# Keys and values of the memory for the last layer: projected in the first mixer instead of the latent-attention stage

## The chip, the cores and the metric

The kernel runs on one core of a Trainium2 chip. The metric is the device time of one execution in microseconds (us), from the median of several runs; less is better. The core has TensorE (PE, matrix products), VectorE (DVE), ScalarE (ACT), GpSimd (POOL) and SyncE (SP, which here only issues DMAs). They run in parallel, each through its own instructions in order, and wait for each other on semaphores.

## The reference

The reference is four transformer layers on a 256 x 1024 activation in float32. The two of the first block: an even mixer (attention with dilated branches and eight heads of 64, beside a state-space scan with a GLU), an odd mixer (gated linear recurrence), a SwiGLU behind each. The two of the second block: latent attention and grouped-query attention, each with a memory attention beside it, a SwiGLU behind each. What the change moves is the memory part of the last layer (i = 1):

```python
mem_n = _rmsnorm(mem, mem_norm)
kv = (mem_n @ w_kv).reshape(B, M, 2, MEM_HEADS, MEM_HEAD_DIM)
k = _rmsnorm(kv[:, :, 0], k_norm)
v = kv[:, :, 1]
```

`mem` (256 x 1024) and `w_kv` (1024 x 1024) are inputs: neither depends on any layer, so k and v can be computed at any time before the last attention.

## The kernel before

Every product is made in three matmuls (`mm3`, L404 to L406): weights and activations are split into a high part and a remainder (`WH` and `WL`; `HTh` and `HTl`, `YAh` and `YAl`, `CTh` and `CTl`), and high x high, high x low and low x high are added in PSUM. All weights stand in one array of chunks of 128 x 2048, in the order of `plan()`. SyncE loads them into three buffers `RAW`; ACT copies a chunk into `WH` (L1015), VectorE subtracts for `WL` (L1588), and there are three buffers of each. On ACT and VectorE `feed(c)` splits the chunks up to c + 3; the split of chunk n waits on ACT until TensorE has used chunk n - 3, and on VectorE until ACT has done its part. `rows_mm` on TensorE goes over the chunks of a matrix (24 matmuls of 512 columns in a full one) and calls a `hook` behind each; `rows_mm` on ACT and VectorE calls `feed`, then the hook.

There is no scheduler: the order on each engine is the order of the code. In the first mixer the chunks are ev_u, ev_q, ev_k, ev_v, and the state scan goes in four groups q = 0 to 3 through the hooks. On VectorE `seg_a(q)` rotates (L1866 to L1874) and then calls `skip(q - 1)` (L1853), and `seg_b(q)` makes the next group's angle table (L1836, L1840), eight scans (L1888, L1889) and four products W (L1893 to L1896). On TensorE `seg_a(q)` is `c_h(q - 1)` (L569 to L574; it waits for the W of that group) and `seg_b(q)` is `b_u(q + 1)` (L557; it waits until VectorE has read the last group's PSUM). On ACT `seg_a` and `seg_b` make angles and sines. Groups 2 and 3 lie within `attention0`: a loop of ten steps in which TensorE makes scores of head h (L621), turns P of head h - 1 and multiplies head h - 2 (L646), with `glu` at step 6; ACT has exp (L1295), gelu at step 4 and the GLU's tanh at step 7. Behind it comes ev_out.

The latent-attention stage runs `mla_a`, `mla_b`, `mla_c`, then `mem10` and `mem11` (keys and values of the memory for the last layer) between the products of the latent projections qb2, qb0 and kvb0; `mem_rows(1)` turns the 256 x 1024 memory on TensorE first, `mem_hi(1)` and `mem_lo(1)` split it into HTh and HTl, `gain_turn` turns the normed keys into `KM`. `qb2` waits for `CTl`, which `c_lo` on VectorE makes behind the feed of mla_c. `power` on GpSimd (L2248) makes each inverse root, in the fixed order of `NAMED_RSTD`.

## Time and profile before

| | us |
|---|---|
| median of 3 runs | 1373.48 (1372.35 to 1377.26) |
| the profiled execution | 1378.56 |
| its span, first to last instruction | 1376.8 |
| TensorE busy in it | 1285.7 |
| VectorE busy | 819.8 |
| ScalarE busy | 680.4 |
| GpSimd busy | 52.0 |
| mean granted clock of TensorE, as a share of 2.4 GHz | 0.971 |

The profile is one execution, and its rows carry the times below. In a timeline a row is a run of like instructions on one engine: start, length, engine, line, operation, output and input, count, and in brackets the idle time before it with who ended it. L12 is line 12 of the kernel. The ends of matmuls are modelled, so the distance of starts is the better measure of their pace. The granted clock is 1.00 at 2.4 GHz and 0.50 at 1.2 GHz.

### The profile page before, as it was taken

What the parts mean: (1) busy time and instruction counts of PE and PEld (TensorE: products, weight loads), DVE (VectorE), ACT (ScalarE), POOL (GpSimd) and SP (SyncE); (2) the same over time, 40 slices, a digit from 0 to 9 for tenths busy, and PEclk for the clock granted to TensorE, in tenths of its full rate; (3) what the DMA queues carried; (4) which work ended last, traced back from release to release, by engine and by line L of the source; (5) the groups of instructions that cost most, each with busy time, mean ns of one, the idle gap of its engine ahead of it and who ended that gap; (6) DMA issues with size and microseconds to landing.
All of it is one profiled execution on the core that took longest, in us unless ns stands there. A gap on an engine that the chain in (4) does not pass through costs nothing.

```text
span 1376.8 us, 15928 instructions
## 1 busy us (share of the span) xinstructions
PE 1285.7 (93%) x6374; PEld 1053.0 (76%) x6374; DVE 819.8 (60%) x1132; ACT 680.4 (49%) x1087; POOL 52.0 (4%) x67
## 2 busy tenths in 40 slices
PE   6888899999998989999999889999999969999998
PEld 5666688888786778888787668788887857788887
DVE  7793565563686675664567543766545664666643
ACT  6444354443568664443488733544435553544431
POOL 0110000000000010000012100000000100000000
PEclk9887999999999999999999899999999989999999
DMA  8330255555543446555455203555554511465551
GB/s 309 120 108 1 95 199 184 185 178 198 188 180 99 177 157 214 189 188 183 155 203 198 88 7 123 184 183 183 184 184 164 183 62 61 153 213 184 184 183 62
DMA packets 31962, 216.62 MB, mean 157 GB/s; under 512 B 3840, under 2 KB 4224, under 8 KB 6672
## 3 DMA queue, kind: packets, MB, share of 16 engines
q1 hardware_dynamic: 30240, 210.29, 43.7%
q0 software_dynamic: 1360, 4.78, 1.1%
q8 instruction: 50, 0.82, 0.2%
q10 hardware_dynamic: 288, 0.52, 0.1%
q14 instruction: 24, 0.20, 0.0%
HBM read 214.54 MB, written 1.05 MB: 157 GB/s over the span
## 4 chain that ended last, share of the span: by engine, by line
PE 76%; DVE 12%; ACT 8%; issue 3%; DMA 1%; POOL 1%; SPq 0%; DVEq 0%; ACTq 0%
PE PS L404 22%; PE PS L406 22%; PE PS L405 22%; PE PS L410 4%; DVE WL L1588 3%; ACT WH L1015 3%; PE PS L676 2%; PE PS L699 2%; ACT JK L1127 1%; ACT HTh L1028 1%; DVE HTl L1602 1%; DMA RAW<-in_w 1%; POOL st L2248 1%; PE PS L557 0%; DVE YG L1633 0%
## 5 line engine op out<-in xcount | busy, mean ns | idle before, releaser
L1588 DVE TENSOR_TENSOR WL<-RAW,WH 128x2048 fp32r<-128x2048 f32 (+1 forms) x200 | 451.1, 2260 | 397.9 <-ACT WH L1015 397.8
L1015 ACT ACTIVATE WH<-RAW 128x2048 fp32r<-128x2048 f32 (+1 forms) x200 | 377.3, 1891 | 443.9 <-PE PS L406 442.2
L404 PE MATMUL PS<-WH,HTh 128*128 128x512 f32 (+2 forms) x1008 | 399.7, 397 | 24.1 <-DVE WL L1588 13.4
L406 PE MATMUL PS<-WH,HTl 128*128 128x512 f32 (+2 forms) x1008 | 393.0, 390 | 0.0
L405 PE MATMUL PS<-WL,HTh 128*128 128x512 f32 (+2 forms) x1008 | 392.4, 389 | 0.0
L404 PEld LDWEIGHTS PS<-WH,HTh 128*128 128x128 f32 x1008 | 191.0, 190 | 64.7 <-DVE WL L1588 25.0
L406 PEld LDWEIGHTS PS<-WH,HTl 128*128 128x128 f32 x1008 | 190.6, 189 | 39.8
L405 PEld LDWEIGHTS PS<-WL,HTh 128*128 128x128 f32 x1008 | 191.2, 190 | 36.7
L404 PE MATMUL PS<-WH,YAh 128*128 128x512 f32 x386 | 153.2, 397 | 1.0 <-DVE WL L1588 0.6
L405 PE MATMUL PS<-WL,YAh 128*128 128x512 f32 x386 | 151.1, 391 | 0.0
L406 PE MATMUL PS<-WH,YAl 128*128 128x512 f32 x386 | 150.9, 391 | 0.0
L404 PEld LDWEIGHTS PS<-WH,YAh 128*128 128x128 f32 x386 | 73.1, 189 | 16.3 <-DVE WL L1588 1.1
L406 PEld LDWEIGHTS PS<-WH,YAl 128*128 128x128 f32 x386 | 73.0, 189 | 15.6
L405 PEld LDWEIGHTS PS<-WL,YAh 128*128 128x128 f32 x386 | 73.1, 189 | 14.7
L2248 POOL TENSOR_TENSOR st<-st,mh 128x2 f32<-128x2 f32 (+4 forms) x33 | 36.2, 1099 | 913.0 <-DVE st L1618 913.0
L1028 ACT ACTIVATE HTh<-PS,cst 128x128 fp32r<-128x128 f32 (+1 forms) x144 | 40.8, 396 | 37.5 <-PE PS L410 37.5
L1602 DVE SCALAR_TENSOR_TENSOR HTl<-PS,cst,HTh 128x128 fp32r<-128x128 f32 (+1 forms) x144 | 41.0, 359 | 14.4 <-ACT HTh L1028 13.9
L1028 ACT ACTIVATE YAh<-PS 128x512 fp32r<-128x512 f32 x38 | 21.6, 584 | 21.5 <-PE PS L410 21.5
L410 PE MATMUL PS<-ident,X 128*128 128x128 f32 x128 | 18.7, 286 | 10.1 <-DMA X<-in_x 5.5
L410 PEld LDWEIGHTS PS<-ident,X 128*128 128x128 f32 x128 | 15.1, 146 | 14.4 <-issue 9.6
L410 PE MATMUL PS<-ident,Z 128*128 128x128 f32 (+1 forms) x124 | 19.3, 291 | 6.3 <-DVE Z L1723 3.6
L410 PEld LDWEIGHTS PS<-ident,Z 128*128 128x128 f32 (+1 forms) x124 | 14.5, 142 | 11.9 <-issue 4.6
(349 smaller groups left out, 1358.2 us busy)
## 6 DMA issues: line engine op xcount, KB each, us to landing
RAW<-in_w SPq DMA_DIRECT2D x197, 1024.0 KB, 4.9
BC<-in_rows POOLq DMA_DIRECT2D x4, 512.0 KB, 3.9
YG<-in_mem POOLq DMA_DIRECT2D x4, 512.0 KB, 5.0
X<-in_x SPq DMA_DIRECT2D x2, 512.0 KB, 6.0
BC<-in_s SPq DMA_DIRECT2D x1, 512.0 KB, 12.7
BB<-in_s SPq DMA_DIRECT2D x1, 512.0 KB, 12.4
YG<-in_s SPq DMA_DIRECT2D x1, 512.0 KB, 13.1
out_x<-X SPq DMA_DIRECT2D x2, 256.0 KB, 2.1
```

The costliest lines, as they stand in the source:

```text
L404: e.matmul(out, ah, bh, start=start, stop=False)
L405: e.matmul(out, ah, bl, start=False, stop=False)
L406: return e.matmul(out, al, bh, start=False, stop=stop)
L410: return e.transpose(out, src, ident[0:p, 0:p])
L676: tk = e.matmul(PS[:, h % 2, 256 * t:256 * t + 256], q[:, 128 * t:128 * t + 128], k[:, 0:256], start=i == 0, stop=i == len(parts) - 1)
L699: tk = e.matmul(PS[:, b, o:o + 128], PT[:, h % 2, kt, 128 * t:128 * t + 128], heads[h]["v"][kt], start=kt == 0, stop=kt == 1)
L1015: e.activation(WH[:, c % NW, w], RAW[:, c % NR, w], ACT.Copy).then_inc(S.hi, 1)
L1028: return e.activation(out, src, ACT.Copy, scale=scale)
L1127: e.activation(JK[:, d * i:d * i + d], z[:, d * i:d * i + d], ACT.Square, accum_out=st[:, SO[name] + nh * n + i:SO[name] + nh * n + i + 1] ...
L1588: e.tensor_tensor(WL[:, c % NW, w], RAW[:, c % NR, w], WH[:, c % NW, w].bitcast(f32), SUB).then_inc(S.lo, 1)
L1602: return e.scalar_tensor_tensor(out, src, gain, hi.bitcast(f32), MUL, SUB)
L2248: e.tensor_tensor(st[:, at:at + n], st[:, at:at + n], mh[:, 0:n], ALU.pow).then_inc(S.rs, 1)
```

## The change

The two projections of the last layer's memory leave the latent-attention stage. In the first mixer `mem` is loaded into the buffer of x (`MX` is X, which has been turned by then and is loaded again later), turned in four rounds of four transposes through one PSUM bank (`mem_round`) behind ev_k, ev_v's first chunk and ev_v, and split into YAh and YAl; `mem10` and `mem11` follow ev_v. The scan's groups 2 and 3 move from the first steps of `attention0` into the hooks of these two, and `attention0` begins when they are through, with gelu ahead of its first exp and glu at step 3 instead of 6. In the latent-attention stage what used `mem10` and `mem11` goes, qb0 comes directly behind qb2, and some banks and buffers change. Buffers W, cosT and PT0 of the scan now lie over KM, VM and BB, which saves the room that KM and VM take up earlier.

The diff, cut to its core. The plan, buffers, and TensorE's part:

```diff
+    for i in range(2):
+        add(f"mem1{i}", nat("w_mem_kv_2", 1, [(512 * i, 512)]))
...
     add("mla_c", nat("mla_w_in_2", 0, [(704, 512)]))
-    add("mem10", nat("w_mem_kv_2", 1, [(0, 512)]))
...
-    add("mem11", nat("w_mem_kv_2", 1, [(512, 512)]))
...
+            MX, KZ1 = X, BC[:, :].rearrange("p (t n) -> p t n", t=2)
...
-            PT0 = sb("A0PT", [128, 2, 2, 256])
+            PT0 = BB[:, :, :, :].rearrange("p r (b q) s -> p r b (q s)", b=2)
...
-        KM, VM = sb("KM", [128, 2, 4, 256]), sb("VM", [128, 2, 2, 512])
...
             def glu():
...
+                e.wait_ge(S.gout, GT["memk1"] + 2)
...
             def attention0():
                 def step(h):
-                    if h == 0:
-                        seg_b(2)
-                    elif h == 1:
-                        seg_a(3)
+                    if h == 1:
+                        gain_turn(KZ1, "memk1", (4, 5), lambda jp: e.wait_ge(S.bread, 4) if jp == 0 else None)
...
-                        c_h(3)
-                    elif h == 6:
...
-                    if h == 0:
-                        e.wait_ge(S.pairs, 6)
-                    if h > 1:
+                    if h < 2:
+                        e.wait_ge(S.kz, h + 1)
+                    else:
...
                 def turn_p(h):
...
-                        e.wait_ge(S.ev, 8)
+                        e.wait_ge(S.vm, h + 1)
...
+            def mem_round(j):
+                if j == 0:
+                    e.wait_ge(S.c_mem, 32)
+                    e.wait_ge(S.k0, 1)
+                else:
+                    e.wait_ge(S.mlo, 2 * j)
+                four(6, MX, j).then_inc(S.mt, 1)
...
+                    mem_round(0)
...
             def behind_v(ci):
...
                     pairs(Qn, (0, 1), q_ready)
+                    mem_round(1)
...
                     pairs(Kn, (0, 1), k_ready)
+                    mem_round(2)
...
             rows_mm(PLAN["ev_v"], 4, 8, 512, HT, (2, 3), v_free, behind_v)
+            mem_round(3)
+            def mem10_ready(k, t):
+                if k == 0:
+                    e.wait_ge(S.pairs, 5 + t)
+                if t == 0:
+                    e.wait_ge(S.mlo, k + 1)
+            def mem11_free(k, t):
+                if k == 0:
+                    e.wait_ge(S.ev, 7 + t)
+            MT = (YAh, YAl)
+            rows_mm(PLAN["mem10"], 4, 8, 512, MT, (0, 1), mem10_ready, lambda ci: seg_a(3) if ci else seg_b(2))
+            rows_mm(PLAN["mem11"], 4, 8, 512, MT, (2, 3), mem11_free, lambda ci: c_h(3) if ci else None)
...
-            mem_rows(1)
             rows_mm(PLAN["mla_c"], 4, 8, 512, HT, (0, 1), evacuated("za"))
...
-            rows_mm(PLAN["mem10"], 4, 8, 512, HT, (0, 1), mem10_ready)
...
             rows_mm(PLAN["qb2"], 3, 3, 512, CQ, (2, 3), qb2_ready)
+            rows_mm(PLAN["qb0"], 3, 3, 512, CQ, (0, 1), evacuated("zc"))
             gain_turn(ZC, "zm", (5, 6))
-            rows_mm(PLAN["mem11"], 4, 8, 512, HT, (0, 1), mem11_free)
...
-            gain_turn(ZD, "memk1", (4, 5), lambda jp: e.wait_ge(S.gout, GT["qmt"] + 1) if jp else e.wait_ge(S.ctl, 5))
-            rows_mm(PLAN["qb0"], 3, 3, 512, CQ, (2, 3), evacuated("z2"))
-            rows_mm(PLAN["kvb0"], 2, 2, 512, CK, (0, 1), kvb0_free, keep=S.kv)
+            e.wait_ge(S.ctl, 5)
+            rows_mm(PLAN["kvb0"], 2, 2, 512, CK, (2, 3), evacuated("z2"), keep=S.kv)
...
             def ready2(h):
-                if h == 4:
+                if h < 2:
+                    e.wait_ge(S.z, ZEV["vt0"] + h + 1)
+                elif h == 4:
```

ACT's part:

```diff
+            def mem_round(j):
+                e.wait_ge(S.mt, j + 1)
+                for k in (2 * j, 2 * j + 1):
+                    tk = copy(YAh[:, k, :], PS[:, 6, 256 * (k % 2):256 * (k % 2) + 256], col("mem_norm_2", k))
+                tk.then_inc(S.mhi, 1)
...
+                    mem_round(0)
+                    mem_squares(0, MX, yq[:, :, :].rearrange("p a b -> p (a b)"))
...
             def behind_v(ci):
...
                     pairs(1, QT, (0, 1), 0.125)
+                    mem_round(1)
...
                     pairs(2, KT, (0, 1))
+                    mem_round(2)
...
+            mem_round(3)
+            rows_mm(PLAN["mem10"], lambda ci: seg_a(3) if ci else seg_b(2))
+            e.wait_ge(S.used, PLAN["mem10"][1] + 1)
+            e.wait_ge(S.rs, RSTD["mem1"])
+            mem_k((0, 1), KZ1)
+            e.wait_ge(S.kz, 2)
+            head_squares("memk1", [KZ1[:, t, :] for t in range(2)], 4, 128, X[:, 0, :])
+            rows_mm(PLAN["mem11"])
+            e.wait_ge(S.used, PLAN["mem11"][1] + 1)
+            mem_v(1, (2, 3))
...
             def attention0():
                 def step(h):
...
-                        seg_b(2)
+                        gelu()
...
-                        seg_a(3)
+                        gain_turn("memk1", lambda j: KM[:, 1, j:j + 2, :], col("memk_norm_2", 1), (4, 5))
...
-                        gelu()
-                    elif h == 7:
...
-                    elif h == 8:
+                    elif h == 6:
...
-            e.wait_ge(S.hsq, HSQ["zk"] + 2)
-            e.wait_ge(S.c_mem, 64)
-            mem_squares(1)
             feed(PLAN["mla_c"][0])
             z_evac("zc", PLAN["mla_c"][1], (0, 1), ZC, 512, True)
-            mem_hi(1)
             feed(PLAN["mla_c"][1])
...
             c_turn(2, (2, 3), 3)
-            e.wait_ge(S.msq, 4)
+            c_turn(3, (4,), 4)
+            e.wait_ge(S.hsq, HSQ["zk"] + 2)
             head_norm("zm", two(ZC), 4, 128, "zc")
...
-            feed(PLAN["mem10"][0])
-            c_turn(3, (4,), 4)
-            e.wait_ge(S.used, PLAN["mem10"][1] + 1)
-            e.wait_ge(S.rs, RSTD["mem1"])
-            mem_k(1, (0, 1), ZD)
-            feed(PLAN["mem10"][1])
-            e.wait_ge(S.kz, 4)
-            e.wait_ge(S.hsq, HSQ["pe"] + 2)
-            head_squares("memk1", two(ZD), 4, 128)
             z_evac("z2", PLAN["qb2"][0], (2, 3), ZB)
             feed(PLAN["qb2"][0])
-            e.wait_ge(S.hsq, HSQ["memk1"] + 8)
+            e.wait_ge(S.hsq, HSQ["pe"] + 2)
             head_norm("qp", two(ZB), 8, 64, "z2")
+            z_evac("z0", PLAN["qb0"][0], (0, 1), ZD)
+            feed(PLAN["qb0"][0])
...
             gain_turn("qmt", lambda j: QMT[:, j:j + 2, :], gq[:, 1:2], (5, 6))
-            feed(PLAN["mem11"][0])
-            e.wait_ge(S.used, PLAN["mem11"][1] + 1)
-            mem_v(1, (0, 1))
-            feed(PLAN["mem11"][1])
...
-            gain_turn("memk1", lambda j: KM[:, 1, j:j + 2, :], col("memk_norm_2", 1), (4, 5))
-            z_evac("z0", PLAN["qb0"][0], (2, 3), ZA)
-            feed(PLAN["qb0"][0])
-            z_evac("zk0", None, (0, 1), ZC, kv=1)
+            z_evac("zk0", None, (2, 3), ZC, kv=1)
```

VectorE's part (`seg_a` has a new argument `between`, called ahead of `skip`):

```diff
+                if ed == 1 and t == 0:
+                    e.wait_ge(S.c_xr, 32)
...
+            def mem_round(j):
+                e.wait_ge(S.mhi, j + 1)
+                for k in (2 * j, 2 * j + 1):
+                    rest(YAl[:, k, :], PS[:, 6, 256 * (k % 2):256 * (k % 2) + 256], YAh[:, k, :], col("mem_norm_2", k)).then_inc(S.mlo, 1)
...
+                if between:
+                    between()
...
-                    seg_a(1)
+                    seg_a(1, mem_first)
+            def mem_first():
+                mem_round(0)
+                mem_var(0, "mem1")
             def behind_v(ci):
...
+                    mem_round(1)
...
-                    seg_a(2)
+                    seg_a(2, lambda: mem_round(2))
+            def behind_mem11(ci):
+                if ci == 0:
+                    seg_b(3)
+                    head_var("memk1", 4, 128)
+                else:
+                    skip(3)
+                    scaled("memk1", [KZ1[:, t, :] for t in range(2)], 4, 128)
...
             rows_mm(PLAN["ev_v"], behind_v)
+            mem_round(3)
+            rows_mm(PLAN["mem10"], lambda ci: seg_a(3) if ci else seg_b(2))
+            rows_mm(PLAN["mem11"], behind_mem11)
...
             def attention0():
                 def step(h):
-                    if h == 0:
-                        seg_b(2)
-                    elif h == 1:
-                        seg_a(3)
-                    elif h == 2:
-                        seg_b(3)
-                    elif h == 3:
-                        skip(3)
+                    if h == 2:
+                        gelu_lo()
...
-                        gelu_lo()
-                    elif h == 8:
...
-                    elif h == 9:
+                    elif h == 7:
...
             feed(PLAN["mla_c"][0])
-            mem_lo(1)
             feed(PLAN["mla_c"][1])
...
             c_lo(2, (2, 3), 3)
+            c_lo(3, (4,), 4)
             head_var("zm", 4, 128)
...
-            feed(PLAN["mem10"][0])
-            c_lo(3, (4,), 4)
-            feed(PLAN["mem10"][1])
-            head_var("memk1", 4, 128)
             feed(PLAN["qb2"][0])
...
-            scaled("memk1", two(ZD), 4, 128)
...
                 rope("qp", ZB[:, t, :], 8, 64, t, tg[:, 0, :, :, :], RP, RQ)
-            feed(PLAN["mem11"][0])
-            feed(PLAN["mem11"][1])
             feed(PLAN["qb0"][0])
...
-            scaled("n0", two(ZA), 4, 128)
+            scaled("n0", two(ZD), 4, 128)
```

GpSimd's part:

```diff
+            e.wait_ge(S.turn, turn_n(0, 1, 1))
+            e.wait_ge(S.rowsq, 2)
+            for t in range(2):
+                e.dma_start(MX[:, t, :], A["mem"][128 * t:128 * t + 128, :]).then_inc(S.c_mem, 16)
...
-            e.wait_ge(S.k0p, 1)
+            power("mem1", 16, 2)
+            power("memk1", SO["memk1"], 8)
+            e.wait_ge(S.mt, 4)
+            e.wait_ge(S.msq, 2)
+            e.wait_ge(S.hsq, HSQ["memk1"] + 8)
+            for t in range(2):
+                e.dma_start(X[:, t, :], A["x"][128 * t:128 * t + 128, :]).then_inc(S.c_xr, 16)
+            e.wait_ge(S.gturn, GT["memk1"] + 2)
...
-            mem_rows()
...
-            power("mem1", 16, 2)
...
-            power("memk1", SO["memk1"], 8)
```

## Rows read from the trace of the kernel before

**Rows 1.** The page's parts 1 and 4: TensorE, and the chain that ended last.
```profile
PE 1285.7 (93%) x6374; PEld 1053.0 (76%) x6374; DVE 819.8 (60%) x1132; ACT 680.4 (49%) x1087; POOL 52.0 (4%) x67
PE 76%; DVE 12%; ACT 8%; issue 3%; DMA 1%; POOL 1%; SPq 0%; DVEq 0%; ACTq 0%
```
**Rows 2.** Windows: length, busy time of each engine, granted clock, DMA share.
```profile
53.90:62.60 8.70, 8.63 (x104) 7.29 (x105) 8.56 (x16) 1.92 (x4) 0.80 (x1) 0.50 0.42 148
83.40:146.10 62.70, 46.27 (x416) 37.02 (x415) 37.80 (x89) 28.57 (x69) 0.00 (x0) 0.72 0.10 35
698.95:700.62 1.67, 1.67 (x19) 1.67 (x17) 0.97 (x2) 1.47 (x3) 0.62 (x1) 1.00 0.99 422
699.00:762.10 63.10, 56.99 (x282) 46.90 (x281) 44.74 (x90) 51.46 (x128) 13.23 (x9) 0.98 0.50 181
714.46:725.44 10.98, 10.98 (x49) 9.04 (x49) 8.57 (x21) 9.72 (x31) 2.30 (x2) 1.00 0.31 108
```
**Rows 3.** Timeline of TensorE in the state scan: start, length, operation, idle before.
```profile
53.85 1.22 PE L557 MATMUL PS<-uT,BBe 32*128 32x128 f32 x8 [5.31 <-DVE JK L1872]
58.01 1.08 PE L543 MATMUL PS<-CFo,BC 128*32 128x32 f32 x64
60.47 0.63 PE L404 MATMUL PS<-WH,HTh 128*128 128x512 f32 x1
60.89 0.63 PE L405 MATMUL PS<-WL,HTh 128*128 128x512 f32 x1
91.02 1.22 PE L557 MATMUL PS<-uT,BBe 32*128 32x128 f32 x8 [2.63 <-DVE JK L1872]
109.14 0.65 PE L569 MATMUL PS<-uT,K 32*32 32x128 f32 x8 [2.40 <-DVE W L1896]
146.11 0.78 PE L404 MATMUL PS<-WH,YAh 128*128 128x512 f32 x1
```
**Rows 4.** Timeline of ACT and VectorE, one round of the scan from 83.48 on.
```profile
83.48 1.91 ACT L1015 ACTIVATE WH<-RAW 128x2048 fp32r<-128x2048 f32 x1 [1.74 <-PE PS L406]
85.43 2.29 DVE L1588 TENSOR_TENSOR WL<-RAW,WH 128x2048 fp32r<-128x2048 f32 x1 [0.34 <-ACT WH L1015]
87.64 0.68 DVE L1866 TENSOR_TENSOR YG<-PS,cosT 128x512 f32<-128x512 f32 x1
91.00 0.69 DVE L1874 TENSOR_TENSOR YG<-YG,JK 128x512 f32<-128x512 f32 x1
92.00 0.42 DVE L1836 TENSOR_SCALAR sinT<-cosT 128x512 f32<-128x512 f32 x1
97.68 0.69 DVE L1896 TENSOR_TENSOR W<-YG,cosT 128x512 f32<-128x512 f32 x1
```
**Rows 5.** Timeline of ACT at gelu, within the first attention.
```profile
116.92 1.06 ACT L1215 ACTIVATE yq<-yq 128x1024 f32<-128x1024 f32 x1
119.08 1.28 ACT L1295 ACT_TABLE_LOAD   x1
```
**Rows 6.** Timeline of the latent-attention stage around mem10, and at qb1.
```profile
711.80 1.26 ACT L1028 ACTIVATE Z<-PS,st 128x512 f32<-128x512 f32 x2 [3.47 <-PE PS L406]
714.46 0.47 PE L404 MATMUL PS<-WH,HTh 128*128 128x512 f32 x1 [1.82 <-DVE HTl L1602]
720.03 1.65 DVE L1602 SCALAR_TENSOR_TENSOR YAl<-PS,cst,YAh 128x256 fp32r<-128x256 f32 x4
763.44 0.99 PE L404 MATMUL PS<-WH,YAh 128*128 128x512 f32 x1
```
**Rows 7.** Timeline of the same stage: norm and rotation of the q parts.
```profile
734.42 1.14 ACT L1121 ACTIVATE JK<-Z 128x512 f32<-128x512 f32 x2
736.77 1.27 DVE L2158 TENSOR_REDUCE st<-JK 128x8 f32<-128x512 f32 x2
738.33 3.27 POOL L2248 TENSOR_TENSOR st<-st,mh 128x16 f32<-128x16 f32 x1 [4.64 <-DVE st L1618]
744.64 0.69 DVE L2121 TENSOR_TENSOR Z<-Z,st 128x512 f32<-128x512 f32 x1
```

More of the change, by code:

```diff
@@ L725, in gain_turn, with mem_rows @@
                     four(bks[jp], src, jp, lambda j, t: e.wait_ge(S.nz, NZ[name] + t + 1) if j == 0 and jp == 0 else None).then_inc(S.gturn, 1)
-            def mem_rows(i, free=None):
-                e.wait_ge(S.c_mem, 32 * (i + 1))
+            def mem_rows(free):
+                e.wait_ge(S.c_mem, 64)
                 for t in range(2):
                     for k in range(8):
-                        if t == 0 and k % 2 == 0 and free:
+                        if t == 0 and k % 2 == 0:
                             free(k // 2)
@@ L951, in tfree2 @@
             def tfree2(h):
-                if h == 0:
-                    e.wait_ge(S.z, ZEV["vt0"] + 2)
-                elif h == 3:
+                if h == 3:
                     e.wait_ge(S.gout, GT["qt1"] + 2)
@@ L1856, in dve, with seg_a @@
             rotated = {}
-            def seg_a(q):
+            def seg_a(q, between=None):
                 C, Sn, A0, A1 = slots(q)
@@ L2076, in mem_norm @@
                 scaled("memk0", [KZ[:, t, :] for t in range(2)], 4, 128)
[L2078 removed]
+            wide_mm(PLAN["od_out"], 3, after=(lambda: mem_var(1, "mem0"), mem_norm))
             ffn(1, 3)
```

91 lines of the change are left out of this document (39 added, 52 removed).

## Prediction

> **What bounds the kernel now.** I read the page first: TensorE is busy for 93% of the span and carries 76% of the chain that ended last [rows 1]. A step that only moves TensorE's work can pay only where TensorE stands still, or runs at the lower of its two clocks. So I cut the span into stages. From 83.4 to 146.1 (the rest of the state scan, and the first attention laid over it) TensorE is busy 46.3 us of 62.7 at a granted clock of 0.72; from 699.0 to 762.1 (the latent-attention stage up to its first products) it is busy 57.0 of 63.1 at 0.98 [rows 2]. In the first there are 16 us of idle to fill, in the second hardly any. Then the timelines, for who is late. In the scan TensorE waits for VectorE: 5.31 us ahead of 53.85, 2.63 ahead of 91.02, 2.40 ahead of 109.14 [rows 3]. VectorE's own order there is a weight remainder (WL), six rotation steps, the table, the scans, four products W, all in one line with no gap [rows 4]. VectorE is the pacer of this stage, and that decides what moved matmuls find there.
>
> **What moves.** Two projections of 48 matmuls each, 11.0 us apiece [rows 2], 16 transposes of `mem` (1.7 us, the same group) and 8 for memk1 (0.9 at the same rate): 24.5 us of TensorE time at full clock. Nothing is saved in total, apart from waits and clock. Both ends must be walked through.
>
> **The scan stage, step by step.** Rates: a 512-column matmul is 0.23 us at 2.4 GHz (10.98 / 48) and 0.43 at 1.2 GHz (60.47 to 60.89) [rows 2, 3]; a chunk is 24 of them, 5.5 or 10.3 us. b_u took 4.2 at the low clock (53.85 to 58.01 [rows 3]), c_h about as much, so 2.1 to 2.3 at the high one. WH takes 1.9, WL 2.2 [rows 4].
> - Two memory rounds of 4 transposes stand ahead of the end of ev_v, 0.5 each: everything from 83.4 on is 1.0 later. ACT gets 4.0 more ahead of Kn's evacuation (squares and two copies); the rope of K on GpSimd then ends near 78.4 against a first use at 84.3, so that is hidden. It would cost at once if Kn came 6 us late.
> - `mem_round(3)` on TensorE waits for the remainders of round 2, and VectorE has these behind WL (86.4) and the rotation (87.64 to 91.69 before [rows 4], so 88.6 to 92.6): they end at 93.5. TensorE has run out at 88.5. This is a new wait of 5.0 us. An idle of 5.31 before left the granted clock at 0.50 for the next 8.7 us [rows 2, 3]. So mem10's first chunk starts at 94.0 and pays 20 matmuls at 0.43 and 4 at 0.23: it ends at 103.5, where 99.5 would be undisturbed.
> - Now the order on VectorE bites. `rows_mm` calls `feed` ahead of the hook, and feed of that chunk splits the chunk three places on, which needs the buffer that this chunk frees. So seg_b(2), which started at 92.0 before, queues behind WH and WL: 103.5 + 4.2 = 107.7, and with its 6.4 us (92.00 to 98.37 [rows 4]) it ends at 114.1. TensorE does b_u(3) and the next chunk meanwhile (2.3 + 5.5, to 111.3) and waits 2.8 for W.
> - c_h(2) 2.3, mem11's first chunk 5.5: 121.9. Again WH and WL (126.1), then seg_b(3), which has no table (1.1 of the 6.4), 5.3: 131.4. TensorE's last chunk ended at 127.4, so it waits 4.0. c_h(3) starts at 131.4; before, it started at 109.14 [rows 3]: 22.3 later.
> - From c_h(3) to the first ev_out matmul are 37.0 us now (109.14 to 146.11 [rows 3]). After the change heads 0 to 3 no longer lie ahead of it (about 4 us more), and gelu, its copy and a table load (116.92 to 120.36, 3.4 us [rows 5]) stand ahead of the first exp; against that no scan step and no gelu interrupt the heads. I take 38, between 33 and 42.
> Scan stage: 22.3 + 1 = **23.3 later**. That is almost all that was moved in: the idle is not filled, it is pushed back.
>
> **The latent-attention stage.** `mem_rows` is gone, so mla_c ends at 709.9 in place of 711.6. What mem10 and mem11 covered is now bare.
> - qb2 needs CTl. ACT evacuates zc (1.2 [rows 6]), splits a chunk (1.9), copies; VectorE has WL in front of c_lo (2.2 and 0.8, half of the four in 1.65 [rows 6]): 709.9 + 1.2 + 1.9 + 2.2 + 0.8 = 716.1, with TensorE out of work at 711.2. A new wait of 4.9, and the clock at 0.50 again: 18 matmuls at 0.43 end qb2 at 723.9.
> - The rotated q parts: evacuation 1.1, WH 1.9, WL 2.2 (the squares, 1.1, run beside it), reductions 1.3, and then the 7.1 from POOL's start to the last product (738.2 to 745.3, of which POOL has 3.3 [rows 7]): 737.5. TensorE has qb0 (4.7, its first matmuls slow), 10 transposes and 12 matmuls (4.0) until 732.6: a second wait of 4.9, of which the trace before shows nothing, because mem11 lay over it.
> - 16 transposes and 12 matmuls follow at the low clock to 746.2. Then ACT: evacuation 1.1, WH 1.9, QTn 1.2, half of KTn 0.6: qb1 starts at 751.0. Before it started at 763.44 [rows 6]: 12.4 gained, and 1.5 more, since qb1 ran its first matmuls at the low clock before (0.99 for the first, against 0.47 for the one at 714.46 [rows 6]).
> This stage: **13.9 earlier**, not 26.
>
> **Sum.** 23.3 - 13.9 = 9.4. The profiled execution took 1378.56 us (span 1376.8), so 1388.0 in its own terms; the median before is 1373.48, 5.1 below that execution, and I put the difference on it: **1383**.
>
> Edits with no price: the DMA of `mem` goes from GpSimd at about 25 us, when 16 transposes of X are done, into X; needed at 67. X is read again and BC's gain row comes only after KZ1 is turned, near 141; first use is in the add behind ev_out, beyond 185. Each of these 1 MB loads costs nothing unless its issue slips by 40 us: GpSimd waits inside power("memk1") until 132, and only these two DMAs are queued behind it. The DMA engines are at 0.10 in the stage [rows 2]. SyncE's queue sees the same chunks in another order. The added waits (kz, vm, gout of memk1, vt0) fall on steps that come later anyway in this schedule.
>
> **The rivals.**
> B, the clock costs nothing. My sum has four stretches at the low clock. Without them mem10's chunk ends 4.0 earlier and c_h(3) takes 2.0 less (stage +17.3), and in the latent stage 3.6 on qb2 and 4.0 behind the second wait go (21.5 earlier): 4.2 net gain, 1369. For it: the wait of 1.82 ahead of 714.46 left the clock at 1.00 [rows 2, 6]. Against it: 5.31 and 2.63 did not, the stage as a whole is at 0.72 [rows 2, 3]. The Trainium skill (TensorE: Matmul & The Clock Gate, What's actually happening) counts the ramp as under 1% of a typical span and advises not to fit to a number of slow matmuls. By that rule rival B's time would hold; the trace shows 8.7 us at 0.50 after one such wait, which speaks against it here.
> C, faster: the heads, no longer cut up by scan steps, run at TensorE's pace. The place is c_h(3) to ev_out. Before, this stage had 16.4 us of idle [rows 2]; if all of it takes in moved work, the stage grows by 24.5 - 16.4 = 8.1 and the sum is 8.1 - 13.9 = -5.8, 1368, and with B's clock in part 1363. It decides once the 38 us shrink below 22. Against it: gelu, glu, tanh and ten head steps still hang on ACT, and the scans still hang on WL. The Trainium skill (Perfetto Trace Analysis, Optimization Strategy) says that interleaving regimes with different contended engines may improve performance. By that rule C would be the outcome; the trace has VectorE without a gap in just this stretch, so I hold it unlikely.
> D, more waits tip the clock. The 2.8 us ahead of c_h(2) is as long as the 2.63 that did it before: c_h(2) 2.1 and mem11's chunk 2.2 more. In the heads VectorE has WL and two steps of glu in front of head 5's mask, about 2.5 of idle and a slow tail, 4 more: 1391.
>
> **How the numbers follow.** Forecast 0.50 (own range 1377 to 1389), B 0.20, C 0.12, D 0.18. Range 1367 to 1394: it takes in B, D, most of C and both ends of the 38. About 0.5% (6.9 us) is what can be told from no change: 1366.6 to 1380.3. Slower: 0.40 of the forecast and all of D, 0.58. Same: 0.10 of the forecast, B, 0.30. Faster: 0.12.
>
> **What would show it.** On TensorE a wait near 5 us ahead of the transposes of round 3, and waits of some 3 and 4 ahead of c_h(2) and c_h(3), all released by VectorE; seg_b(2)'s scans directly behind a WL; c_h(3) near 131. The first ev_out matmul near 169 to 170. In the later stage two waits near 5 us, ahead of qb2 and of the transposes of the q parts, each followed by a clock of 0.50; the stage shorter by 14 at its end. I am wrong if seg_b(2) starts before mem10's first chunk ends, if ev_out starts before 160, or if either of the two later waits is missing.

## Result and profile after

| | before | after |
|---|---|---|
| median, same chip (4 runs each) | 1375.14 us | 1390.35 us (1388.71 to 1390.78) |
| ratio | 1 | 1.011, 95% interval 1.0086 to 1.0133 |
| profiled execution, its span | 1378.56, 1376.8 | 1390.78, 1389.0 |
| TensorE busy, mean granted clock | 1285.7, 0.971 | 1291.2, 0.965 |

The change costs 15.2 us by the medians and 12.2 between the spans of the two profiled executions. First TensorE's timeline of the kernel after (start, length, operation, idle before and who ended it), as rows 3 and 6 show it of before:

```profile
92.06 1.11 PE L412 MATMUL PS<-ident,X 128*128 128x128 f32 x4 [4.63 <-DVE YAl L1613]
92.82 0.77 PE L406 MATMUL PS<-WH,YAh 128*128 128x512 f32 x1
100.96 0.73 PE L559 MATMUL PS<-uT,BBe 32*128 32x128 f32 x8
111.79 0.65 PE L571 MATMUL PS<-uT,K 32*32 32x128 f32 x8 [2.73 <-DVE VM L1916]
131.32 0.65 PE L571 MATMUL PS<-uT,K 32*32 32x128 f32 x8 [4.54 <-DVE VM L1916]
140.21 0.84 PE L412 MATMUL PS<-ident,Kn 128*128 128x128 f32 x3 [1.89 <-ACT Kn L1323]
162.50 1.11 PE L412 MATMUL PS<-ident,YG 128*128 128x128 f32 x4 [3.08 <-ACT BB L1038]
175.34 0.78 PE L406 MATMUL PS<-WH,YAh 128*128 128x512 f32 x1
...
745.64 0.77 PE L406 MATMUL PS<-WH,YAh 128*128 128x512 f32 x1 [5.27 <-DVE YAl L1613]
762.84 0.30 PE L412 MATMUL PS<-ident,Z 128*64 128x128 f32 x1 [2.83 <-DVE Z L2149]
765.77 3.41 PE L412 MATMUL PS<-ident,Z 128*64 128x128 f32 x15 [2.63 <-DVE Z L2149]
777.45 0.77 PE L406 MATMUL PS<-WH,YAh 128*128 128x512 f32 x1 [2.19 <-ACT KTn L1038]
```

Every wait of the scan ends on a VectorE operation. Read from the top: round 3's transposes wait for the remainders of round 2; the moved chunk starts; c_h(2) and c_h(3) (the operations that begin with `uT,K`) wait for W, which now lies in VM's memory. c_h(3) starts at 131.32 (109.14 before [rows 3]), ev_out at 175.34 (146.11 before [rows 3]). So the first ev_out matmul is 29.2 later. VectorE's timeline says why:

```profile
84.95 2.29 DVE L1599 TENSOR_TENSOR WL<-RAW,WH 128x2048 fp32r<-128x2048 f32 x1
91.14 0.87 DVE L1613 SCALAR_TENSOR_TENSOR YAl<-PS,cst,YAh 128x256 fp32r<-128x256 f32 x2
103.07 2.29 DVE L1599 TENSOR_TENSOR WL<-RAW,WH 128x2048 fp32r<-128x2048 f32 x1 [8.11 <-ACT WH L1025]
105.28 0.42 DVE L1854 TENSOR_SCALAR sinT<-KM 128x512 f32<-128x512 f32 x1
106.42 0.42 DVE L1908 TENSOR_TENSOR_SCAN YG<-s,YG 128x128 f32<-128x128 f32 x1
...
123.39 2.29 DVE L1599 TENSOR_TENSOR WL<-RAW,WH 128x2048 fp32r<-128x2048 f32 x1 [5.17 <-ACT WH L1025]
125.59 0.42 DVE L1908 TENSOR_TENSOR_SCAN YG<-s,YG 128x128 f32<-128x128 f32 x1
```

The engine that paces the scan stands still for 8.11 and 5.17 us. What it waits for is a half of a weight chunk that may be split only when the moved chunk has freed its buffer, and the table and the scans of group 2 (105.28, 106.42) and group 3 (125.59) are queued behind that. Before, the table of group 2 ran at 92.00 [rows 4].

Windows of the kernel after (length; busy time of PE, PEld, DVE, ACT, POOL; granted clock; DMA share and GB/s): the scan up to c_h(3), from there to ev_out, the stretch behind the wait of 3.08, and the one behind the wait of 5.27.

```profile
83.40:131.32 47.92, 35.05 (x284) 27.83 (x283) 32.07 (x53) 21.99 (x41) 0.00 (x0) 0.87 0.26 89
131.32:175.34 44.02, 36.78 (x241) 29.80 (x241) 17.61 (x48) 20.05 (x57) 5.25 (x4) 0.69 0.24 84
162.50:180.10 17.60, 16.93 (x60) 13.96 (x61) 4.76 (x14) 5.53 (x17) 0.00 (x0) 0.50 0.01 5
745.60:750.20 4.60, 4.55 (x11) 3.62 (x12) 2.98 (x11) 1.78 (x12) 2.29 (x2) 0.51 0.65 228
```

The heads run at 0.69, and from 162.5 to 180.1 TensorE is busy 16.9 of 17.6 us at the low clock. The latent-attention stage, from its first matmul to out0's first, went from 146.15 (681.39 to 827.54) to 129.95 (710.65 to 840.60): 16.2 shorter. 29.2 - 16.2 = 13.0, against 12.2 between the spans.

### The profile page after: what moved, and what is told of

It is laid out like the page before. It is cut to its first block, busy times and chain, and to the rows that moved or that the text cites. A ratio compares the mean times of both kernels' runs of the same rounds, so it can differ in the third digit from the quotient of the medians.

```text
span 1389.0 us, 15929 instructions
## 1 busy us (share of the span) xinstructions
PE 1291.2 (93%) x6374; PEld 1057.3 (76%) x6374; DVE 819.5 (59%) x1132; ACT 680.7 (49%) x1086; POOL 55.4 (4%) x69
## 4 chain that ended last, share of the span: by engine, by line
PE 77%; DVE 11%; ACT 7%; issue 2%; POOL 1%; DMA 0%; SPq 0%; DVEq 0%; ACTq 0%
PE PS L406 23%; PE PS L408 23%; PE PS L407 23%; PE PS L412 4%; DVE WL L1599 3%; ACT WH L1025 3%; PE PS L675 2%; PE PS L698 1%; ACT HTh L1038 1%; ACT JK L1137 1%; POOL st L2268 1%; DVE HTl L1613 1%; DMA RAW<-in_w 0%; PE PS L645 0%; DVE YG L1644 0%
## 5 line engine op out<-in xcount | busy, mean ns | idle before, releaser
L406 PE MATMUL PS<-WH,HTh 128*128 128x512 f32 (+2 forms) x976 | 387.2, 397 | 20.2 <-DVE WL L1599 12.6
L408 PE MATMUL PS<-WH,HTl 128*128 128x512 f32 (+2 forms) x976 | 380.7, 390 | 0.0
L407 PE MATMUL PS<-WL,HTh 128*128 128x512 f32 (+2 forms) x976 | 380.4, 390 | 0.0
L406 PEld LDWEIGHTS PS<-WH,HTh 128*128 128x128 f32 x976 | 185.0, 190 | 59.4 <-DVE WL L1599 23.3
L406 PE MATMUL PS<-WH,YAh 128*128 128x512 f32 x418 | 168.9, 404 | 7.8 <-DVE YAl L1613 5.3
L407 PE MATMUL PS<-WL,YAh 128*128 128x512 f32 x418 | 166.1, 397 | 0.0
L408 PE MATMUL PS<-WH,YAl 128*128 128x512 f32 x418 | 165.9, 397 | 0.0
L406 PEld LDWEIGHTS PS<-WH,YAh 128*128 128x128 f32 x418 | 81.0, 194 | 25.3 <-DVE WL L1599 5.5
L408 PEld LDWEIGHTS PS<-WH,YAl 128*128 128x128 f32 x418 | 80.6, 193 | 17.5
L407 PEld LDWEIGHTS PS<-WL,YAh 128*128 128x128 f32 x418 | 81.0, 194 | 16.5
L412 PE MATMUL PS<-ident,X 128*128 128x128 f32 x144 | 21.8, 291 | 12.8 <-DMA X<-in_x 5.1
L412 PEld LDWEIGHTS PS<-ident,X 128*128 128x128 f32 x144 | 17.4, 148 | 17.6 <-issue 7.6
L412 PE MATMUL PS<-ident,Z 128*128 128x128 f32 (+1 forms) x116 | 18.3, 298 | 8.3 <-DVE Z L2149 5.5
```

Source lines behind the costliest of these rows:

```text
L406: e.matmul(out, ah, bh, start=start, stop=False)
L407: e.matmul(out, ah, bl, start=False, stop=False)
L408: return e.matmul(out, al, bh, start=False, stop=stop)
L412: return e.transpose(out, src, ident[0:p, 0:p])
```

## Experiments

All marks below are starts on TensorE in the profiled execution. Four orders that could be to blame were changed one by one (e1 to e4), then the clock and the heads were tested. All edits are against the changed kernel, but for e12's, which is against the kernel before. `finish`, named below, is the step behind four heads in which TensorE turns their result; the first stands within head 5.

| kernel | median us | c_h(2) | c_h(3) | ev_out | c_h(3) to ev_out |
|---|---|---|---|---|---|
| before | 1375.14 | 98.51 | 109.14 | 146.11 | 37.0 |
| after | 1390.35 | 111.79 | 131.32 | 175.34 | 44.0 |
| e1 scan ahead of the split | 1382.01 | 108.39 | 121.73 | 166.22 | 44.5 |
| e2 glu behind mask 5 | 1388.38 | 111.38 | 130.84 | 174.25 | 43.4 |
| e3 remainders ahead | 1382.92 | 104.87 | 124.25 | 167.84 | 43.6 |
| e4 latent copies ahead | 1386.09 | 111.10 | 130.65 | 174.62 | 44.0 |
| e5 all four | 1373.60 | 102.65 | 115.99 | 159.89 | 43.9 |
| e6 matmuls in the scan's waits | 1384.54 | 109.10 | 127.10 | 169.18 | 42.1 |
| e7 glu late | 1392.07 | 110.83 | 128.81 | 175.51 | 46.7 |
| e8 matmuls at finish | 1384.88 | 110.53 | 128.56 | 169.37 | 40.8 |
| e9 heads ahead | 1384.57 | 112.16 | 131.74 | 168.91 | 37.2 |
| e10 what paid, together | 1363.50 | 102.36 | 116.79 | 149.71 | 32.9 |
| e11 and the latent waits | 1358.40 | 102.32 | 116.75 | 148.15 | 31.4 |
| e12 before, matmuls in waits | 1369.08 | 97.52 | 109.85 | 140.35 | 30.5 |

**e1: the order on VectorE.**

```diff
-            rows_mm(PLAN["mem10"], lambda ci: seg_a(3) if ci else seg_b(2))
-            rows_mm(PLAN["mem11"], behind_mem11)
+            seg_b(2)
+            feed(PLAN["mem10"][0])
+            seg_a(3)
+            feed(PLAN["mem10"][1])
+            behind_mem11(0)
+            feed(PLAN["mem11"][0])
+            feed(PLAN["mem11"][1])
+            behind_mem11(1)
```

> The changed kernel with one thing reordered: on VectorE and ScalarE the scan steps of groups 2 and 3 are issued ahead of the weight split that the moved chunk triggers, not behind it. TensorE's instructions are untouched. Theory (the split is in front of the scan in VectorE's order, and it waits for the moved chunk): seg_b(2) runs at about 95 to 101, c_h(2) loses its wait of 2.7, and c_h(3) starts when TensorE has done the last moved chunk, near 122.5 and with no wait, where it was 131.3; the first ev_out matmul comes near 166.5 (was 175.3), and the time is about 1381.5 against the changed kernel's 1390.4. Rival (the moved work itself, 24.5 us of matmuls, is what fills the stage): c_h(3) stays within 2 us of 131 and the time within 2 of 1390. Rival (the heads behind it are the bound): c_h(3) moves, but ev_out by less than 3.

Measured: 1382.01 (ratio to before 1.0045, 1.0029 to 1.0061). TensorE's and VectorE's timelines of e1:

```profile
108.39 0.43 PE L571 MATMUL PS<-uT,K 32*32 32x128 f32 x8
121.73 0.43 PE L571 MATMUL PS<-uT,K 32*32 32x128 f32 x8
...
96.67 0.42 DVE L1911 TENSOR_TENSOR_SCAN YG<-s,YG 128x128 f32<-128x128 f32 x1
102.47 2.29 DVE L1602 TENSOR_TENSOR WL<-RAW,WH 128x2048 fp32r<-128x2048 f32 x1 [0.56 <-ACT WH L1025]
```

Both waits are gone, no bracket stands at either c_h, the wait of VectorE for WH is 0.56 instead of 8.11, and c_h(3) comes 9.6 earlier with the same matmuls ahead of it. That settles the order on VectorE as the cause of that part, and falsifies "the moved work itself". c_h(3) to ev_out stays about as it was (44.5 against 44.0), so nearly all of the gain arrives: ev_out is 9.1 earlier and the median 8.3 lower.

**e3: the wait ahead of round 3.** In `seg_a(2)` the call of `mem_round(2)` on VectorE moves from behind the rotation to ahead of it:

```diff
+                if q == 2:
+                    between()
                 e.wait_ge(S.bu, q + 1)
...
-                if between:
+                if between and q == 1:
                     between()
```

> The changed kernel with the two remainders of memory round 2 put ahead of VectorE's rotation of group 2, not behind it. Theory: the transposes of round 3 wait some 1.5 in place of 4.6, the clock does not fall for the moved chunk behind them (2.6 more), and since the split and with it seg_b(2) hang on that chunk's end, all of it arrives: c_h(3) near 125.8 (was 131.3), ev_out near 170, time 1385. If the clock costs nothing, only 3 of it: 1387.5. If VectorE's pace alone sets the scan, the rotation is 1.7 later and nothing is gained: 1390 to 1392.

Measured: 1382.92 (1.0052, 1.0036 to 1.0068).

```profile
87.98 0.66 PE L412 MATMUL PS<-ident,X 128*128 128x128 f32 x4 [0.66 <-DVE YAl L1613]
104.87 0.65 PE L571 MATMUL PS<-uT,K 32*32 32x128 f32 x8 [2.73 <-DVE VM L1918]
124.25 0.43 PE L571 MATMUL PS<-uT,K 32*32 32x128 f32 x8 [4.55 <-DVE VM L1918]
```

The wait went from 4.63 to 0.66, and the waits ahead of the two c_h stayed as they were, only earlier: c_h(2) and c_h(3) moved together, by 6.9 and 7.1. Of the 6.9, 4.1 are the earlier start of round 3, and 2.8 come behind it, where the chunk now runs at the full clock (16.9 us from round 3 to c_h(2), 19.7 before). VectorE hangs on the end of the moved chunk, as the theory has it; its own pace would have moved nothing.

**e2 and e7: where the glu stands.** e2 moves VectorE's part from step 5 to step 6; e7 puts TensorE's part to step 6, ScalarE's to 7 and 8, VectorE's to 8 and 9, where the kernel before has them.

```diff
-                    elif h == 5:
+                    elif h == 6:
                         feed(PLAN["glu"][0])
```

e7, on TensorE:

```diff
-                    elif h == 3:
+                    elif h == 6:
                         glu()
```

> The changed kernel with VectorE's part of the glu (a weight remainder and two products, 3.6 us) put behind head 5's mask, not ahead of it. Theory (these steps hold back head 5's mask, at 160.4, and with it the division and the transposes of finish at 162.5, behind which the clock falls): mask 5 comes at about 157, the wait of 3.1 ahead of finish is under 1, and ev_out starts 3 earlier (172) with the time near 1387.5. Rival (the heads hang on ScalarE's exp and TensorE's transposes in turn, and the steps are merely passed on to head 6): finish comes earlier, head 6's mask does not, and ev_out moves by less than 1, time 1390.

> The changed kernel with the glu put back where the kernel before had it among the heads (TensorE's step 6, ScalarE's 7 and 8, VectorE's 8 and 9), everything else as changed. Theory (the heads hang on ScalarE and TensorE in turn, wherever the glu stands, and 44 us is eight heads, gelu and glu at the low clock): ev_out at 174 to 175, within 1.5 of the changed kernel, time 1389 to 1391. Rival (an early glu is what made c_h(3) to ev_out 44 and not 38): ev_out near 169.5 and the time near 1385.

Measured: 1388.38 (1.0095, 1.0078 to 1.0112) and 1392.07 (1.0128, 1.0107 to 1.0149). TensorE in e2, and a window behind the first of these rows:

```profile
159.15 1.14 PE L412 MATMUL PS<-ident,YG 128*128 128x128 f32 x4 [0.61 <-DVE YG L1968]
167.32 1.09 PE L412 MATMUL PS<-ident,Kn 128*128 128x128 f32 x3 [1.88 <-ACT Kn L1323]
174.25 0.78 PE L406 MATMUL PS<-WH,YAh 128*128 128x512 f32 x1
159.15:167.00 7.85, 6.29 (x21) 4.39 (x21) 5.62 (x10) 1.86 (x4) 0.00 (x0) 0.50 0.27 83
```

finish comes 3.4 earlier, as expected, but a new wait of 1.88 opens one head later and ev_out gains 1.1. For e2 my theory falls: ev_out had to come 3 earlier. The rival, less than 1, is missed by 0.1, and the time lies between the two. One thing more stands in the window: the wait ahead of finish is only 0.61 here, and the clock behind it is 0.50 all the same. In the changed kernel, too, it was down as the 3.08 us wait began (a mean of 0.53 over 159.42:162.50). So that wait did not drop it; what did is not shown. In e7 ev_out comes at 175.51, 0.2 later than in the changed kernel and half a us outside my 174 to 175, and the time is 1.1 over my 1391. c_h(3) to ev_out is 2.7 longer (46.7). An early glu is not what made the 44; it rather helped.

**e4: the first wait of the latent stage.** `feed(PLAN["mla_c"][1])` moves behind the three `c_turn` on ScalarE and the three `c_lo` on VectorE:

```diff
-            feed(PLAN["mla_c"][1])
             c_lo(1, (0, 1), 2)
             c_lo(2, (2, 3), 3)
             c_lo(3, (4,), 4)
+            feed(PLAN["mla_c"][1])
```

> The changed kernel with, in the latent-attention stage, the copies and remainders of the turned latents (ScalarE and VectorE) issued ahead of the weight split of mla_c's second chunk, not behind it. Theory: the wait ahead of qb2 is 1.2 in place of 5.3, the clock stays up through qb2 (2.2 more), and out0 starts 4 to 6 earlier relative to the stage's start: time near 1385. Rival: the later wait, ahead of the transposes of the rotated q parts, takes it over, since VectorE then has the split and the pe rotation in front of the q parts: out0 moves by less than 2, time 1389 to 1390.

Measured: 1386.09 (1.0074, 1.0056 to 1.0093), 4.3 under the changed kernel.

```profile
741.64 0.47 PE L406 MATMUL PS<-WH,YAh 128*128 128x512 f32 x1 [1.99 <-DVE YAl L1613]
759.05 0.30 PE L412 MATMUL PS<-ident,Z 128*64 128x128 f32 x1 [3.48 <-DVE Z L2149]
```

5.27 became 1.99, where 1.2 was expected. qb2's first matmul takes 0.47 instead of 0.77, at the high clock, but the clock did not stay up: 0.8 us later the matmuls are 0.43 apart, as at the low one, until 745.8. The next wait took 0.65 of the gain (2.83 to 3.48). From the stage's start to the first matmul of the attention's output projection (out0) are 126.75 us (709.91 to 836.66) in place of 129.95. That is 3.2 shorter, between the 4 to 6 of my theory and the 2 of the rival.

**e5: the four together.**

> The changed kernel with all four reorderings at once (scan steps ahead of the split, glu steps behind head 5's mask, round 2's remainders ahead of the rotation, latent copies ahead of the split). Alone they came out 8.3, 2.0, 7.4 and 4.3 us under the changed kernel's 1390.35. Theory (the first and the third take away different waits: the one in front of the moved matmuls, the other behind them): they add up, TensorE is busy without a wait from round 3 to c_h(3), which starts near 115.5; ev_out starts near 159.5, and the time is 1370, from 1368 to 1373, so below the kernel before. Rival (both buy the same slack on VectorE, whose own work then sets the scan): c_h(3) near 120 and the time 1376 to 1378.

Measured: 1373.60 (0.9988, 0.9976 to 0.9999; 10 runs). c_h(3) is at 115.99, and in the scan TensorE is busy 30.96 of 32.59 us at full clock. c_h(3) is where the theory put it, near 115.5, so e1 and e3 took away two different waits. The whole gain is less than the sum: 16.8 us where the four alone make 22.0, and 0.6 over the upper end of my range. And this is only level with the kernel before: c_h(3) to ev_out is still 43.9.

```profile
83.40:115.99 32.59, 30.96 (x288) 24.89 (x286) 31.95 (x53) 17.83 (x37) 1.97 (x1) 1.00 0.29 98
115.99:159.89 43.90, 35.76 (x242) 28.66 (x241) 17.73 (x49) 24.40 (x61) 3.28 (x4) 0.70 0.30 108
```

**e6 and e8: the price of the low clock.** Matmuls whose result nothing reads are put into waits, so TensorE does not stand still while every wait of the real work stays.

```diff
+            def spin(n, b):
+                for _ in range(n):
+                    e.matmul(PS[:, b, 256:512], HTh[:, 0, 0:128], HTh[:, 0, :], start=True, stop=True)
...
+                if j == 3:
+                    e.wait_ge(S.pairs, 5)
+                    spin(36, 0)
...
+                if q > 1:
+                    e.wait_ge(S.ssm, q)
+                    spin((20, 34)[q - 2], 7)
```

The first pair stands in TensorE's `mem_round`, the second in `c_h`; e8 has 26 of the same in `finish(0)` alone.

> The changed kernel with idle matmuls that nothing reads (128 x 256 columns, 0.11 us each at full clock) put into three waits of the scan: 36 ahead of the transposes of round 3, 20 ahead of c_h(2), 34 ahead of c_h(3). No wait of the real work changes. Theory (the clock falls because TensorE stands still, and costs what the rows at 0.43 against 0.23 us say): the moved chunk behind the first wait ends 2.6 earlier, c_h(2) is 1.6 shorter, c_h(3) and the turns behind it 2: c_h(3) starts near 127 (was 131.3), ev_out near 169 to 170, and the time is 1384 to 1385. Rival (the clock costs nothing, since the time between is VectorE's): ev_out moves by less than 1.5, time 1389 to 1390.

> The changed kernel with 26 idle matmuls (128 x 256, 0.11 us each) in one wait alone, the 3.1 us ahead of the transposes of finish in head 5. Behind that wait TensorE works 12 us with hardly a gap at the low clock (162.5 to 174.5), and ev_out's first ten matmuls too. Theory (this one wait costs the clock of all that follows): TensorE's part behind it shrinks by up to half, the heads then hang on ScalarE, and ev_out starts 3 to 5 earlier and is itself 2 quicker at its start: time 1384 to 1386. Rival (the clock falls again at the next short wait, the heads being too thin to hold it): ev_out within 1.5 and the time 1389 to 1391.

Measured: 1384.54 (1.0072, 1.0048 to 1.0096) and 1384.88 (1.0077, 1.0055 to 1.0099). First e6 from round 3 to c_h(3), then e8: behind the filled wait (window 160:174, against 162.50:180.10 above), in it, and the rows at its ends:

```profile
92.00:127.10 35.10, 34.08 (x259) 28.78 (x259) 23.72 (x42) 16.41 (x30) 0.00 (x0) 1.00 0.26 91
```
```profile
160.00:174.00 14.00, 13.23 (x79) 10.71 (x79) 4.58 (x14) 5.52 (x17) 0.00 (x0) 0.99 0.01 2
156.90:160.40 3.50, 3.50 (x19) 3.50 (x19) 2.26 (x8) 1.42 (x6) 0.00 (x0) 0.51 0.79 293
156.51 4.84 PE L653 MATMUL PS<-HTh 128*128 128x256 f32 x26
161.19 0.60 PE L412 MATMUL PS<-ident,YG 128*128 128x128 f32 x4
```

The real work runs at 1.00 and 0.99 where it ran at the low clock. In e6 c_h(3) comes 4.2 earlier (2.8 from round 3 to c_h(2), 1.5 from c_h(2) to c_h(3)) and ev_out 6.2.

In e8 the idle matmuls did not hold the clock. It was at 0.51 for 3.5 us among them, and back at full speed when the real work came. So slowed, the 26 took 4.84 us and outlasted the wait: finish starts 32.6 us behind c_h(3), where it was 31.2. From finish to ev_out are then 8.2 in place of 12.8, so that c_h(3) to ev_out shrinks from 44.0 to 40.8; and from ev_out's first matmul to the next stage's are 24.2 in place of 26.4 (175.34 to 201.75). Together that is 5.4, beside 5.5 between the medians. In this one execution c_h(3) was also 2.8 earlier, which is not from the edit: 1.2 of it arose between round 3 and c_h(2), and 1.5 behind c_h(2), where this execution kept the clock up after the wait of 2.73. The low clock behind finish thus costs at least 5.4 us, and rival B is out.

**e9: the heads ahead of c_h(3).** Products of heads 0 and 1 between mem11's chunks, masks behind seg_b(3), exps ahead of gelu.

```diff
-            rows_mm(PLAN["mem11"], 4, 8, 512, MT, (2, 3), mem11_free, lambda ci: c_h(3) if ci else None)
+                rows_mm(PLAN["mem11"], 4, 8, 512, MT, (2, 3), mem11_free, lambda ci: c_h(3) if ci else (products(0), products(1)))
...
+            exps(0)
+            exps(1)
...
+                    masks(0)
+                    masks(1)
```

> The changed kernel with the first two heads laid over the scan again, as the kernel before had them: products of heads 0 and 1 between mem11's two chunks on TensorE, their masks behind seg_b(3) on VectorE, their exps behind the evacuation of VM on ScalarE, at the price of one more table load each way. c_h(3) stays at 131.3 (after c_h(2), 18.0 or 19.5 us as the clock falls or not). Theory (the 44 us from c_h(3) to ev_out are long because no head lies ahead of c_h(3) any more, and gelu with its copy and table load, 3.4 us, stands ahead of the first exp): the transposes of head 0 follow c_h(3) directly, at 135.6 where they came at 140.2, and ev_out starts 3 to 4 earlier: c_h(3) to ev_out 40 to 41, time 1386.5 to 1387.5. Rival (gelu on ScalarE and the pace of the later heads absorb it): c_h(3) to ev_out over 43 and the time 1389 to 1390.5.

Measured: 1384.57 (1.0062, 1.0038 to 1.0086).

```profile
131.74 0.43 PE L571 MATMUL PS<-uT,K 32*32 32x128 f32 x8 [3.46 <-DVE VM L1922]
136.55 0.30 PE L412 MATMUL PS<-ident,BC 128*128 128x128 f32 x1 [1.28 <-DVE BC L1747]
168.91 0.78 PE L406 MATMUL PS<-WH,YAh 128*128 128x512 f32 x1
```

A window of the early heads in e9, then one of the changed kernel:

```profile
136.50:150.00 13.50, 13.21 (x97) 11.52 (x98) 3.58 (x14) 8.94 (x20) 0.53 (x1) 1.00 0.43 156
142.30:149.30 7.00, 6.90 (x28) 5.80 (x29) 0.93 (x6) 3.01 (x14) 0.00 (x0) 0.52 0.02 6
```

c_h(3) stays (0.4 later), and from it to ev_out are 37.2 us, 6.8 less than in the changed kernel; I had expected 40 to 41. So nearly all of the excess of 7 us over the kernel before goes when two heads lie ahead of c_h(3) again and gelu no longer stands in front of the first exp. Which of the two carries more was not separated, nor was the clock: in the changed kernel TensorE is busy for 7 us at 0.52 among the early heads, where e9 runs at 1.00. At twice the clock these 7 us would be 3.4 shorter (an estimate from the window), so up to half of the 6.8 may be the clock.

**e10 and e11: a better version.** e10 is e1, e3, e4, e8 and e9 together, with mem11's last split moved to head 3; e11 adds idle matmuls in two waits of the latent stage. On VectorE e10 has, beyond the others,

```diff
             behind_mem11(0)
             feed(PLAN["mem11"][0])
-            feed(PLAN["mem11"][1])
             behind_mem11(1)
...
                         gelu_lo()
+                    elif h == 3:
+                        feed(PLAN["mem11"][1])
```

and e11, ahead of the transposes of row tile t of the q parts,

```diff
+                            e.wait_ge(S.z, ZEV["z0"] + 2)
+                            for _ in range((30, 22)[t]):
+                                e.matmul(PS[:, 1, 256:512], HTh[:, 0, 0:128], HTh[:, 0, :], start=True, stop=True)
```

> All that has paid, in one kernel: scan steps ahead of the split, round 2's remainders ahead of the rotation, latent copies ahead of the split, idle matmuls in the wait ahead of finish, heads 0 and 1 laid over mem11, and mem11's last split moved from ahead of the skip to head 3. From the 1373.6 of the four reorderings: 3.5 for the heads, 2 for the split ahead of the skip, 4 for the clock, less the 1 that the moved glu steps had bought: 1365 (1362 to 1369), below the kernel before by 0.5 to 0.9%. Rival (the heads hang on ScalarE, which has the same work in any order): c_h(3) to ev_out over 41 and the time over 1370.

> The same with idle matmuls (128 x 256) in two waits of the latent-attention stage as well, 30 ahead of the transposes of the rotated q parts of the first row tile (a wait of 3.5) and 22 ahead of those of the second (2.6). If the low clock costs there what it costs in the scan, the 16 transposes take 1.8 in place of 3.4 and the next 12 matmuls are up to 0.5 quicker: 2 us below the run without them. If VectorE or ScalarE set the pace of that part, under 0.7.

Measured: 1363.50 (0.9904, 0.9873 to 0.9935) and 1358.40 (0.9877, 0.9853 to 0.9901). Windows from qb2 to qb1, first e10, then e11:

```profile
716.02:747.88 31.86, 23.59 (x106) 18.80 (x107) 22.76 (x48) 26.27 (x78) 8.80 (x5) 0.84 0.31 105
```
```profile
714.19:743.94 29.75, 27.12 (x159) 22.47 (x159) 22.76 (x48) 25.74 (x78) 8.80 (x5) 1.00 0.33 115
```

The filled waits bring the 2 us that were expected (31.86 to 29.75). The 5.1 between the medians are more than that. Another 1.5 is the heads, where the two kernels have the same instructions: in e10's profiled execution the clock fell within the 26 idle matmuls ahead of finish, as in e8, and they took 4.69 us; in e11's it stayed up and they took 3.35. One of e10's four executions did as well as e11's (1357.18, at a mean clock of 0.986, where the other three are at 0.975 to 0.977). So a part of the 5.1 is the state of the clock and not the edit. e11 is 1.2% faster than the kernel before.

**e12: does that need the move?** The kernel before, with the same idle matmuls in `b_u(3)`, `c_h`, two `turn_p` and the last `pv`:

```diff
+                if q > 1:
+                    spin((14, 20)[q - 2], (6, 7)[q - 2])
                 e.wait_ge(S.w, 4 * q + 4)
```

> The kernel BEFORE the change, nothing moved, with idle matmuls (128 x 256, 0.11 us each) in six waits of its scan and heads: 22 ahead of b_u(3), 14 ahead of c_h(2), 20 ahead of c_h(3), 28 and 10 ahead of the transposes of heads 4 and 7, 22 ahead of the last product with V. It asks how much of what the best version of the changed kernel gains (1358.4, 18 us under the kernel before) needs the move at all. Theory (the low clock is a cost of its own in both, and the move pays the rest by filling waits): the stage from 83.4 to ev_out, 62.7 us at a clock of 0.72, gets 7 to 9 shorter (c_h(3) 3 earlier, the heads 4 to 5, ev_out's start 1), time 1366 to 1369. Rival 1 (the clock is all there is): 1360 or under. Rival 2 (here VectorE and ScalarE set the pace and the clock is nothing): 1373 or over.

Measured: 1369.08 (0.9956, 0.9938 to 0.9974).

```profile
97.52 0.43 PE L577 MATMUL PS<-uT,K 32*32 32x128 f32 x8 [2.13 <-DVE W L1909]
109.85 0.43 PE L577 MATMUL PS<-uT,K 32*32 32x128 f32 x8
140.35 0.47 PE L404 MATMUL PS<-WH,YAh 128*128 128x512 f32 x1
```

c_h(1) to ev_out went from 60.9 (85.24 to 146.11) to 56.0 (84.33 to 140.35): 4.9, where I expected 7 to 9. No bracket stands at c_h(3), which is 0.7 later than before: the 20 idle matmuls there ran at the low clock in part, took 3.70 us and outlasted the wait, so this is no optimum. The idle matmuls alone give the unmoved kernel 0.4%, 1369.08 at the upper end of my 1366 to 1369; the moved one, put in order, is 10.7 us under that. What idle matmuls in the unmoved kernel's latent stage would add was not tried.

## Why the prediction was right, and where it was off

The sign, the mechanism of the scan and the whole range held: 1390.35 lies within 1367 to 1394. But it is 7.4 over the forecast of 1383, outside the forecast's own 1377 to 1389, and next to rival D's 1391. The 7.4 are made up of 5.9 in the scan stage (29.2 for 23.3), -2.3 in the latent stage, 1.7 by which the median before came out higher (1375.14 for 1373.48), and 2.2 outside both stages.

- Wait ahead of round 3: 5.0 forecast, 4.63. Ahead of c_h(2): 2.8, 2.73. Ahead of c_h(3): 4.0, 4.54. seg_b(2)'s scans stand behind a WL. c_h(3): 131.4 forecast, 131.32. e1 shows the cause.
- That c_h(3) was met to 0.1 us is luck: two errors cancelled. c_h(2) came at 111.79, 2.3 ahead of the 114.1 that I had, mostly because chunk 1 started 1.2 earlier (the 1.0 for the first memory rounds did not show, c_h(1) starts at 85.12 after 85.24) and took 8.1 (92.82 to 100.96) and not 9.5. And c_h(3) followed 19.5 behind c_h(2), where I had 17.3: 1.5 of that is c_h(2) at the low clock after its 2.73, as rival D had it, though the chunk behind it did not run so. I had priced the low clock of chunk 1 at 4.0; e3 and e6 make it 2.8.
- The term that failed is the tail: 38 us from c_h(3) to ev_out, 44.0 measured. I had priced the lost overlap of four heads at about 4 and gelu ahead of the first exp at 3.4, and set against them that no scan step interrupts the heads. e9 takes back 6.8 (44.0 to 37.2) with two heads and gelu's place; whether the saving that I set against them is real, no run shows. The clock is in the 6.8 and was in none of my terms here. Rival D named the place and a size of 4. Its mechanism, glu ahead of mask 5, is worth 1.1 at ev_out (e2); the slow tail that it also named is real, 5.4 with ev_out's own start (e8).
- For rival C I wrote that VectorE has no gap in just this stretch. That is so from 83.4 to 98.4, where it is busy 14.35 of 15.00 us, and wrong for C's place: from 109.14 to 146.11 it is busy 12.92 of 36.97, and TensorE's longest waits there, 3.42 and 2.62, end on ScalarE.
- Latent stage: 13.9 forecast, 16.2 measured. qb2's wait was 4.9 forecast, 5.27; the q parts' was one of 4.9, and is 2.83 + 2.63 = 5.46, cut in two by one transpose. Only 11 of qb2's matmuls were slow where I had 18, and I had missed a third wait, 2.19 ahead of qb1, with a low clock behind it. Again the stretches at the low clock were sized from one example. At qb1's first matmul I had forecast 12.4, and it is 15.2 (82.05 us behind the stage's start, now 66.80).
- Base: I put the sum on the median. The sum of the measured stages is 13.0 and the spans differ by 12.2, but the medians by 15.2: the profiled execution of before was 3.4 over its median (1378.56, 1375.14), that of after 0.4. The clock is the likely reason: on record the executions of before at a mean clock of 0.971 took 1377.5 to 1379.2, as the profiled one, and those at 0.974 or more 1372.1 to 1376.6. Where in the kernel that arises was not looked at.
- The edits without a price: GpSimd's queue and both 1 MB loads released nothing that waited in the rows above.

Rival C did not come: it needed the 38 to shrink under 22. Even e11 has 31.4.

The Trainium skill (TensorE: Matmul & The Clock Gate, What's actually happening) puts the ramp at under 1% of a typical span. In size the runs agree: filling one wait brought 5.5 us (e8), filling three 5.8 (e6), of some 1390. But the whole change is 1.1%, so here it can't be left out. A second page of the Trainium skill, Perfetto Trace Analysis (Optimization Strategy), holds that interleaving regimes with different contended engines may pay. As built the move lost; in e10 and e11, with VectorE's own steps ahead of the splits, it gained, e11 10.7 us against e12. Some of that is the filled waits of the latent stage, which e12 does not have.
